# A recurrent decoder step on one core: decay by an exponential on ScalarE, gated mLSTM output in two parts, gate rows a unit later, sample tile scaled on ScalarE

## The chip, the core and the metric

The kernel runs on one core of a Trainium2 chip. The metric is the device time of one launch in microseconds. The core's engines work side by side, each through its own queue of instructions in order: TensorE (PE; its weight loads are listed as PEld), VectorE (DVE), ScalarE (ACT), GpSimd (POOL) and SyncE (SP), which here only issues transfers. They meet through semaphores: an instruction waits until a named counter has reached a value.

## The reference

One layer of a hybrid recurrent decoder for 512 prompt positions and for 8 samples of 4 positions each, 544 columns in all, in fp32. The core of it:

```
xn = rmsnorm(x, norm_mix_g);  proj = xn @ w_in + b_in      # split into q, k, v, ... gates
# GLA: chunked linear attention, decays exp(cumsum(lg)); o_gla = head_rmsnorm(o) * silu(gg)
# mLSTM: conv, silu, q/k/v block projections, stabilised memory; o_m = head_rmsnorm(hm) * sigmoid(mo)
# RG-LRU:
xc = causal_dwconv(rx);  r, i = sigmoid(blockdiag(xc, w_r) + b_r), sigmoid(blockdiag(xc, w_i) + b_i)
log_a = 8 * r * log_sigmoid(lam);  a = exp(log_a)
bx = sqrt(-expm1(2 * log_a)) * (i * xc);  h_t = a_t * h_(t-1) + bx_t;  o_r = h * gelu(ry)
mix = g0 * (o_gla @ wb0) + g1 * (o_m @ wb1) + g2 * (o_r @ wb2)      # g = sigmoid(gates)
x = x + mix @ w_out
x = x + (gelu(u_a) * u_b) @ w_down,   u = dwconv(rmsnorm(x) @ w_up)
```

The outputs are y for prompt and samples after a last RMSNorm, and the new states of every branch.

## The kernel before, in words

Activations lie with features on partitions and the 544 positions along the free axis. The dense products run as numbered **units**, one for each 128 output features: unit 0 (16 + 4 + 4 small columns: GLA rank, input and forget gates), 1 to 8 (q, k, v of GLA), 9 to 12 (mLSTM input), 13 to 20 (RG-LRU), 21 to 24 (`gg`), 25 to 28 (`mo`), 29 to 52 (gate and branch products, GLA, then RG-LRU, then mLSTM), then w_out, w_up, w_down. A unit takes fp32 products in three passes of a split in two parts: ScalarE rounds a weight tile from `stage` to `whi` (`hi`, L1060), GpSimd subtracts to get `wlo` (`lo`, L505), and TensorE adds up `whi`*`xh` + `whi`*`xl` + `wlo`*`xh` (`gemm`, L581). Two `stage` slots alternate; SyncE loads them as `lo` frees them. ScalarE evacuates each unit's result (`evac`).

The recurrent work is cut into small steps and hung between units by hand: `plan(u, part, ...)` (L303 to L341) names the steps that TensorE, ScalarE and VectorE each run when they come past unit u. Every engine runs its own function for a step, or `nothing`. Part 1 of a unit from 29 on lies between its gate product and its branch product, part 0 behind the unit.

What the change touches:

- **Start** (`start`, L595): TensorE multiplies the identity with itself 18 times, then normalises and transposes x by multiplying each token tile with a diagonal of inverse root mean squares (`normalised`, L601), for four of the eight feature tiles. The other four are scaled in place (ScalarE L1097 for token tiles 0 and 1, VectorE L1565 for 2, 3 and the 32-row sample tile 4) and transposed later (`turned`, L619). VectorE's next work is `xl` (L1572), from the `xh` that ScalarE wrote (L1109). Unit 0 (L634) follows.
- **GLA preparation** (`gprep`: VectorE L1686 to L1712, ScalarE L1188) at unit 8, with the load of the GLA states on ScalarE's queue ahead of it; **gate rows** (`rows`, VectorE L1645 to L1679) at unit 5, their store (`rowst`) at 7, their transposes (`rowt`, TensorE L666, VectorE L1681, ScalarE's exponentials L1177) at 9. The first GLA chunk (`gA`, unit 10) waits for `ke`, `cols` and `ecol`.
- **RG-LRU passes** (`rg`, i = 0 to 3, units 24, 26, 28, 30): TensorE's two gate products (L783), ScalarE two sigmoids, Tanh (L1263) and Sqrt (L1264), VectorE (`v_rg`, L1817) the decay a = (1 - t)/(1 + t) by an addition, a reciprocal and a fused pass (L1827 to L1829), then the input term, the scan and the output gate. ScalarE's sigmoids wait for the previous pass's output (`rg_o`). `mixed` (L1978, L1983) adds the branch products and comes behind the passes on VectorE's queue. The query and key projections (`mqk`, L804) wait for the convolutions and for the last state rows, all behind the passes.
- **mLSTM output** (`mfin`, L1953): in the last slot of unit 44, after the sample columns' normalised output has been copied to `mq`, VectorE multiplies each of four heads by its norm gain and `mo` (L1957), rounds it to `omh` (L1961) and subtracts to `oml` (L1962). Units 45 to 52 take k tiles one by one as `om` counts them. `omh` lies where the sample states' transposes `cts` were, so the second step waits for the last state store. The steps `sH` and `sI` (h = 0 to 3) in units 40 to 44 update the sample states. SyncE waits for `om` before it loads the residual x again (L440).

Of the kernel before, what the change touches and what calls it, by code (L numbers as in the profile page):

```python
# [57 lines left out]
WARM = 18  # L58
# [31 lines left out]
def layer(nc, io):  # L90
    ctx = ExitStack()
    with ctx:
# [58 lines left out]
        gsm = at("gsm", [P, 2, P], o + 6 * TB + 3072)  # L151
        ogh = at("ogh", [P, H, T], o, F32R)
# [32 lines left out]
        cts = at("cts", [P, NB, P + 1], w0)  # L185
        kwb = at("kwb", [TS, NB, P], w0 + 4128)
# [44 lines left out]
        m0s = sml[0:4, 196:204]  # L231

# [116 lines left out]
        def _(sp):  # L349
# [71 lines left out]
            for n in range(3):  # L421
# [143 lines left out]
        def _(pe):  # L565
# [29 lines left out]
            def start():  # L595

                pe.wait_ge(s("ident"), 1)
                for _ in range(WARM):
                    mm(bank(7)[:, 256:384], ident[:], ident[:], start=True, stop=True)
# [16 lines left out]
                pe.wait_ge(s("scaled0"), 2)  # L616
                pe.wait_ge(s("scaled1"), 3)
# [415 lines left out]
        def _(act):  # L1033
# [70 lines left out]
            hi(0)  # L1104

# [71 lines left out]
            def v_rows(_):  # L1177
# [3 lines left out]
                func(ecol[0:TS, 4, :], cols[0:TS, 4, 32:100], ACT.Exp).then_inc(s("ecol"), 1)  # L1181

# [5 lines left out]
            def v_gprep(_):  # L1188
                act.wait_ge(s("out"), outs[0])
                for h in range(H):  # L1190
                    act.dma_start(ss[64 * (h % 2):64 * (h % 2) + 64, h // 2], io["state_gla_S"][0].rearrange("b h k v -> h k b v")[h])\
                       .then_inc(s("ss_in"), 16)
# [59 lines left out]
            def v_rg(i):  # L1252
# [264 lines left out]
        def _(dve):  # L1517
# [86 lines left out]
            def v_a2(_):  # L1604
# [33 lines left out]
                v.scalar_tensor_tensor(out=c4, in0=lp, scalar=8.0, in1=lz2, op0=ALU.mult, op1=ALU.add).then_inc(s("c4"), 1)  # L1638

# [46 lines left out]
            def v_gprep(_):  # L1686

                dve.wait_ge(s("evac"), U_MU)
# [17 lines left out]
                v.tensor_tensor(qk[:, 2:4, :], qk[:, 2:4, :], g1[:], ALU.mult).then_inc(s("ke"), 1)  # L1706
                dve.wait_ge(s("ke"), 1)
# [109 lines left out]
            def v_rg(i):  # L1817
# [358 lines left out]
```

## Time and profile before

| | us |
|---|---|
| runs (median, lowest, highest of 3) | 1016.35, 1015.52, 1017.73 |
| the profiled execution | 1019.24 |
| its span, first to last instruction | 1017.5 |
| busy: TensorE, VectorE, ScalarE, GpSimd | 981.0, 588.2, 401.6, 259.4 |

The profile is one execution. Busy time of an engine is the time in which any of its instructions ran; an idle time is put down to the event that ended it ("releaser"). PEclk is the share of full clock that TensorE was granted: 1.00 is 2.4 GHz, 0.50 is 1.2 GHz. Line numbers are those of the kernel before.

### The profile page before, as it was taken

The page shows a single profiled execution, that of the slowest core. Times are in us where ns is not written, and L with a number is a line of the kernel's source. Part 1 is how long each engine was busy: PE and PEld are TensorE (multiplying, and loading weights), DVE is VectorE, ACT ScalarE, POOL GpSimd, SP SyncE. Part 2 cuts the span into 40 slices and gives each one's busy share as a digit, 9 for nine tenths or more (in the row PEclk, how much of TensorE's full clock was granted, in tenths as well). Part 3 has the DMA queues.
Part 4 walks back from the last instruction along what each step waited for, and adds up shares of the span by engine and source line. Part 5 has one row for each costly group of instructions (what it writes and reads, how often), then busy time and mean ns, then how long its engine had stood idle before and what let it go on. Part 6 is the DMA issues. An engine that isn't in the chain of part 4 may idle for free.

```text
span 1017.5 us, 19211 instructions
## 1 busy us (share of the span) xinstructions
PE 981.0 (96%) x7548; PEld 954.0 (94%) x7548; DVE 588.2 (58%) x902; ACT 401.6 (39%) x579; POOL 259.4 (25%) x145
## 2 busy tenths in 40 slices
PE   7999999998889999998999999999999999999995
PEld 7999999897789999897999999999999999999995
DVE  5484334269973555667545678776777777423132
ACT  5643333456453555222332344444444444222121
POOL 2443222232222231331433230010000100233330
PEclk8999999999999999999999999999999999999998
DMA  5236223243122222523422532233222323432212
GB/s 145 63 101 138 82 64 80 57 123 95 43 66 71 63 62 64 144 73 94 149 82 62 93 88 83 82 93 92 82 82 87 98 83 98 116 93 86 85 57 88
DMA packets 171816, 89.31 MB, mean 88 GB/s; under 512 B 13594, under 2 KB 169888, under 8 KB 171767
## 3 DMA queue, kind: packets, MB, share of 16 engines
q1 hardware_dynamic: 154341, 79.16, 28.1%
q10 hardware_dynamic: 17426, 9.47, 3.5%
q8 instruction: 35, 0.57, 0.3%
q14 instruction: 14, 0.11, 0.0%
HBM read 82.29 MB, written 6.32 MB: 87 GB/s over the span
## 4 chain that ended last, share of the span: by engine, by line
PE 84%; DVE 9%; issue 3%; ACT 1%; POOL 1%; DMA 0%; ACTq 0%; DVEq 0%; POOLq 0%
PE ps L581 74%; PE ps L570 2%; DVE rt L1828 1%; PE ps L804 1%; POOL wlo L505 1%; PE ps L885 1%; PE ps L889 1%; DVE mq L1957 1%; PE ps L634 1%; PE ps L823 1%; DVE rt L1829 1%; DMA xtok<-x_prompt 0%; DVE rt L1531 0%; PE ps L819 0%; DVE gv L1802 0%
## 5 line engine op out<-in xcount | busy, mean ns | idle before, releaser
L505 POOL TENSOR_TENSOR wlo<-stage,whi 128x1024 fp32r<-128x1024 f32 (+2 forms) x77 | 229.9, 2986 | 499.4 <-ACT whi L1060 382.1
L581 PE MATMUL ps<-xh,whi 128*128 128x272 f32 x1536 | 323.5, 292 | 3.7 <-ACT sg L1385 2.5
L581 PE MATMUL ps<-xh,wlo 128*128 128x272 f32 x1536 | 318.1, 289 | 0.0
L581 PE MATMUL ps<-xl,whi 128*128 128x272 f32 x1536 | 317.5, 288 | 0.0
L581 PEld LDWEIGHTS ps<-xh,whi 128*128 128x128 f32 x1536 | 243.1, 189 | 7.8 <-issue 4.4
L581 PEld LDWEIGHTS ps<-xl,whi 128*128 128x128 f32 x1536 | 242.2, 189 | 0.0
L581 PEld LDWEIGHTS ps<-xh,wlo 128*128 128x128 f32 x1536 | 240.5, 189 | 0.0
L1060 ACT ACTIVATE whi<-stage 128x1024 fp32r<-128x1024 f32 (+2 forms) x59 | 72.6, 1230 | 166.5 <-PE ps L581 161.2
L1069 ACT ACTIVATE whi<-stage 128x1024 fp32r<-128x1024 f32 (+1 forms) x54 | 59.9, 1110 | 145.9 <-PE ps L581 141.3
L554 POOL COPY up<-fst 128x16 f32 (+1 forms) x44 | 23.6, 538 | 231.3 <-DVE ca L2061 228.4
L2061 DVE SCALAR_TENSOR_TENSOR ca<-up,par,ca 128x560 f32<-128x560 f32 x88 | 70.3, 799 | 6.1 <-DVE ca L2061 3.2
L581 PE MATMUL ps<-hh,whi 128*128 128x272 f32 x352 | 73.5, 290 | 0.0
L581 PE MATMUL ps<-hl,whi 128*128 128x272 f32 x352 | 72.7, 287 | 0.0
L581 PE MATMUL ps<-hh,wlo 128*128 128x272 f32 x352 | 72.6, 287 | 0.0
L2051 DVE TENSOR_TENSOR wlo<-stage,whi 128x1024 fp32r<-128x1024 f32 (+1 forms) x44 | 54.7, 1244 | 10.0 <-ACT whi L1069 7.8
L2101 DVE TENSOR_TENSOR yb<-xt,ps 128x544 f32<-128x544 f32 x8 | 5.8, 721 | 88.6 <-PE ps L581 88.6
L581 PEld LDWEIGHTS ps<-hl,whi 128*128 128x128 f32 x352 | 55.5, 188 | 0.0
L581 PEld LDWEIGHTS ps<-hh,wlo 128*128 128x128 f32 x352 | 55.0, 188 | 0.0
L581 PEld LDWEIGHTS ps<-hh,whi 128*128 128x128 f32 x352 | 54.9, 188 | 0.1
L2041 DVE TENSOR_TENSOR up<-ps,rstd 128x272 f32<-128x272 f32 x44 | 19.4, 442 | 52.9 <-PE ps L581 52.9
L1385 ACT ACTIVATE sg<-ps,par 128x544 f32<-128x544 f32 x24 | 17.2, 715 | 66.7 <-PE ps L581 55.7
L1445 ACT ACTIVATE ca<-up,par 128x560 f32<-128x560 f32 x44 | 37.7, 857 | 4.0 <-DVE up L2043 2.6
(413 smaller groups left out, 1354.0 us busy)
## 6 DMA issues: line engine op xcount, KB each, us to landing
stage<-w_in SPq DMA_DIRECT2D x52, 512.0 KB, 3.9
stage<-w_up SPq DMA_DIRECT2D x44, 512.0 KB, 3.7
stage<-w_down SPq DMA_DIRECT2D x16, 704.0 KB, 4.6
stage<-w_branch SPq DMA_DIRECT2D x24, 256.0 KB, 4.2
stage<-w_out SPq DMA_DIRECT2D x8, 512.0 KB, 4.0
ch<-state_mlstm_C ACTq DMA_DIRECT2D x4, 512.0 KB, 4.1
s_mlstm_C<-ch ACTq DMA_DIRECT2D x4, 512.0 KB, 3.2
xp<-x_prompt SPq DMA_DIRECT2D x1, 2048.0 KB, 7.7
```

Source lines behind the costliest of these rows:

```text
L505: pool.tensor_tensor(wlo[:, slot, 0:kt], stage[:, slot, 0:kt], whi[:, slot, 0:kt].bitcast(F32), ALU.subtract).then_inc(s("lo"), 1)
L554: pool.tensor_copy(fsam(row[:, FPW:PADF])[:, :, 0:FW - 1], fs).then_inc(s("pads"), 1)
L570: return nc.tensor.transpose(out, in_, ident[0:k, 0:k])
L581: ins = mm(dst[:, r, :], w[:, slot, k0 + k, :], x(k)[:, r * HT:(r + 1) * HT], start=first and k == 0 and q == 0, stop=last and k == n - 1 ...
L634: ins = mm(halves(0)[:, r, :], w[:, 0, k, :], x[:, k, r * HT:(r + 1) * HT], start=k == 0 and q == 0, stop=k == KD - 1 and q == 2)
L1060: func(whi[:, slot, 0:kt], stage[:, slot, 0:kt], ACT.Copy).then_inc(s("hi"), 1)
L1069: func(whi[:, slot, 0:kt], stage[:, slot, 0:kt], ACT.Copy).then_inc(s("hi"), 1)
L1385: func(split(sg[:]), halves(0), ACT.Sigmoid, bias=col).then_inc(s("gate_ev"), 1)
L1445: func(ca[:, r, 0:CONVF], up[:, r, 0:CONVF], ACT.Identity, scale=par[:, bass.ds(j + (P_FW + NF * r), 1)], bias=par[:, bass.ds(j + (P_FB + ...
L2041: v.tensor_tensor(row[:, FW - 1:FW - 1 + HT], src[:, 0, :], rstd[:, 0:HT], ALU.mult)
L2051: v.tensor_tensor(wlo[:, slot, 0:kt], stage[:, slot, 0:kt], whi[:, slot, 0:kt].bitcast(F32), ALU.subtract)\
L2061: v.scalar_tensor_tensor(out=out, in0=row[:, t:t + CONVF], scalar=par[:, bass.ds(j + (P_FW + 2 * NF * t + NF * r), 1)], in1=out, op0=ALU.m ...
```

## The change

- Start: ScalarE scales the sample tile (`scaled(4)`, behind `hi(0)`), VectorE no longer does; TensorE multiplies the identity by itself 4 more times before the third token tile and 6 more times ahead of the last sample tile; unit 0 loads and writes 68 columns instead of 128.
- `gprep` moves from unit 8 to 5 (its first wait becomes q and k evacuated), `rows` from 5 to 6, `rowst` from 7 to 8, and the copies of sample columns become a step `smp` at unit 9. The GLA state loads move behind the exponentials of unit 9.
- RG-LRU: the decay is Exp(-2 c r) on ScalarE between Tanh and Sqrt; VectorE's addition, reciprocal and fused pass go.
- mLSTM output: the 512 prompt columns of head h are gated in a new step `mfp`, one each behind sH(0), sI(0), sH(1), sI(1); `mfin` keeps the 32 sample columns. `cts` and `kwb` move to the memory of `ogh`. `om` is counted once.

```diff
-        cts = at("cts", [P, NB, P + 1], w0)
-        kwb = at("kwb", [TS, NB, P], w0 + 4128)
+        cts = at("cts", [P, NB, P + 1], og0)
+        kwb = at("kwb", [TS, NB, P], og0 + 4128)
+        c8 = sml[:, 204:208]
...
-        plan(5, 0, ("rows", 0))
-        plan(7, 0, ("rowst", 0))
-        plan(8, 0, ("gprep", 0))
-        plan(9, 0, ("rowt", 0))
+        plan(5, 0, ("gprep", 0))
+        plan(6, 0, ("rows", 0))
+        plan(8, 0, ("rowst", 0))
+        plan(9, 0, ("rowt", 0), ("smp", 0))
...
+        for h in range(H):
+            seq[3 * NMC + 1 + h].append(("mfp", h))
...
-                    sp.wait_ge(s("om"), H)
+                    sp.wait_ge(s("om"), 1)
+                    sp.wait_ge(s("ch_out"), 64)
...
+                def warm(n, b=7):
+                    for _ in range(n):
+                        mm(bank(b)[:, 256:384], ident[:], ident[:], start=True, stop=True)
...
+                warm(18)
...
                         tr(bank(7)[:, 128:128 + KD], graw[:], KD).then_inc(s("par_tr"), 1)
+                        warm(4, 1)
                     pe.wait_ge(s("diag"), t + 1)
                     for j in range(4):
+                        if (j, t) == (3, 4):
+                            warm(6)
                         ins = normalised(j, t)
...
-                pe.wait_ge(s("scaled0"), 2)
-                pe.wait_ge(s("scaled1"), 3)
+                pe.wait_ge(s("scaled0"), 3)
+                pe.wait_ge(s("scaled1"), 2)
...
-                            ins = mm(halves(0)[:, r, :], w[:, 0, k, :], x[:, k, r * HT:(r + 1) * HT],
+                            ins = mm(halves(0)[0:68, r, :], w[:, 0, k, 0:68], x[:, k, r * HT:(r + 1) * HT],
...
-                            lambda: None, ready="om")
+                            lambda: pe.wait_ge(s("om"), 1))
...
             hi(0)
+            scaled(4)
...
                 func(ecol[0:TS, 4, :], cols[0:TS, 4, 32:100], ACT.Exp).then_inc(s("ecol"), 1)
+                act.wait_ge(s("out"), outs[0])
+                for h in range(H):
+                    act.dma_start(ss[64 * (h % 2):64 * (h % 2) + 64, h // 2], io["state_gla_S"][0].rearrange("b h k v -> h k b v")[h])\
+                       .then_inc(s("ss_in"), 16)
...
-                act.wait_ge(s("c4"), 1)
-                then(func(rt[2][:, 0:CONVM], rt[2][:, 0:CONVM], ACT.Tanh, scale=c4[:, i:i + 1]))
-                func(rt[4][:, 0:CONVM], rt[2][:, 0:CONVM], ACT.Sqrt).then_inc(s("rg_u"), 1)
+                act.wait_ge(s("c4"), 2)
+
+                func(rt[4][:, 0:CONVM], rt[2][:, 0:CONVM], ACT.Tanh, scale=c4[:, i:i + 1]).then_inc(s("rg_t"), 1)
+                act.wait_ge(s("rg_t"), 2 * i + 1)
+                func(rt[2][:, 0:CONVM], rt[2][:, 0:CONVM], ACT.Exp, scale=c8[:, i:i + 1]).then_inc(s("rg_t"), 1)
+                func(rt[4][:, 0:CONVM], rt[4][:, 0:CONVM], ACT.Sqrt).then_inc(s("rg_u"), 1)
...
+                dve.wait_ge(s("c4"), 1)
+                v.tensor_scalar(c8, c4, -2.0, None, ALU.mult).then_inc(s("c4"), 1)
...
-                dve.wait_ge(s("evac"), U_MU)
+                dve.wait_ge(s("evac"), U_QKV + 4)
...
+                dve.wait_ge(s("rg_copied"), i + 1)
+                v.tensor_tensor(h, h, xc, ALU.mult)
+                dve.wait_ge(s("rg_t"), 2 * i + 2)
                 dve.wait_ge(s("rg_u"), i + 1)
+                then(v.scalar_tensor_tensor(out=b, in0=a, scalar=1.0, in1=b, op0=ALU.add, op1=ALU.mult))
+                then(v.tensor_tensor(b, b, h, ALU.mult))
                 if i:
                     dve.wait_ge(s("or"), i)
-                then(v.tensor_scalar(r, a, 1.0, None, ALU.add))
-                then(v.reciprocal(r, r))
-                then(v.scalar_tensor_tensor(out=a, in0=a, scalar=1.0, in1=r, op0=ALU.subtract, op1=ALU.mult, reverse0=True))
-                v.tensor_tensor(h, h, xc, ALU.mult)
-                then(v.scalar_tensor_tensor(out=b, in0=b, scalar=2.0, in1=r, op0=ALU.mult, op1=ALU.mult))
-                then(v.tensor_tensor(b, b, h, ALU.mult))
...
+            def v_mfp(h):
+                if h == 0:
+                    dve.wait_ge(s("evac"), U_GB)
+                    dve.wait_ge(s("m3_copied"), NMC)
+                q = slice(0, SEQ)
+                then(gated(h, q))
+                then(v.tensor_copy(omh[:, h, q], mq[:, h, q]))
+                v.tensor_tensor(oml[:, h, q], mq[:, h, q], omh[:, h, q].bitcast(F32), ALU.subtract)
...
+                q = slice(SEQ, T)
                 for h in range(H):
-                    then(v.scalar_tensor_tensor(out=mq[:, h, :], in0=mq[:, h, :], scalar=par[:, P_MG + h:P_MG + h + 1],
-                                                in1=mo[:, h, :], op0=ALU.mult, op1=ALU.mult))
-                    if h == 0:
-                        dve.wait_ge(s("stored"), 3)
-                    then(v.tensor_copy(omh[:, h, :], mq[:, h, :]))
-                    v.tensor_tensor(oml[:, h, :], mq[:, h, :], omh[:, h, :].bitcast(F32), ALU.subtract).then_inc(s("om"), 1)
+                    ins = gated(h, q)
+                then(ins)
+                then(v.tensor_copy(omh[:, :, q], mq[:, :, q]))
+                v.tensor_tensor(oml[:, :, q], mq[:, :, q], omh[:, :, q].bitcast(F32), ALU.subtract).then_inc(s("om"), 1)
```

`gated(h, q)` is the product of L1957 on the columns q. `scaled(t)` is the copy of L1097 for token tile t.

## Rows read from the trace of the kernel before

**Rows 1.** The page's part 1: busy us, share of the span, instructions.

```profile
PE 981.0 (96%) x7548; PEld 954.0 (94%) x7548; DVE 588.2 (58%) x902; ACT 401.6 (39%) x579; POOL 259.4 (25%) x145
```

**Rows 2.** Waits of PE: line, releaser: total us, times, longest us.

```profile
PE ps L581 <- DVE mix L1983: 4.0, 1, 4.0
PE ps L804 <- issue: 3.1, 1, 3.1
PE ps L581 <- ACT sg L1385: 2.5, 1, 2.5
PE ps L581 <- DVE oml L1962: 2.2, 3, 0.9
PE ps L634 <- DVE xl L1572: 2.1, 1, 2.1
...
PE ps L570 <- ACT ecol L1181: 1.8, 1, 1.8
```

**Rows 3.** Windows: busy us (instructions) of PE, PEld, DVE, ACT, POOL; PEclk, DMA share, GB/s.

```profile
18.20:25.00 6.80, 6.80 (x29) 5.95 (x28) 2.34 (x4) 2.14 (x3) 0.93 (x5) 0.50 0.33 92
209.00:300.00 91.00, 78.17 (x551) 73.75 (x551) 84.11 (x101) 49.80 (x59) 26.32 (x9) 0.96 0.31 83
267.40:270.70 3.30, 3.30 (x14) 3.30 (x15) 2.83 (x4) 3.25 (x5) 0.00 (x0) 0.50 0.00 0
294.70:298.00 3.30, 3.30 (x10) 2.55 (x9) 3.14 (x10) 3.14 (x6) 0.00 (x0) 0.50 0.02 6
482.40:485.70 3.30, 3.30 (x15) 3.30 (x16) 1.34 (x2) 1.49 (x1) 0.03 (x1) 0.50 0.61 205
```

**Rows 4.** Timeline of the start: start us, us, engine, line, instruction [idle before <-releaser].

```profile
1.61 5.65 PE L599 MATMUL ps<-ident 128*128 128x128 f32 x36 [1.61 <-POOL ident L499]
...
13.23 2.77 DVE L1565 TENSOR_SCALAR xtok<-xtok,sml 32x512 f32<-32x512 f32 x1
13.23 2.35 POOL L505 TENSOR_TENSOR wlo<-stage,whi 128x1024 fp32r<-128x1024 f32 x1 [11.67 <-ACT whi L1060]
...
14.18 2.53 ACT L1109 ACTIVATE xh<-ps,par 128x544 fp32r<-128x544 f32 x4 [1.03 <-PE ps L603]
...
16.83 0.49 PE L634 MATMUL ps<-xh,whi 128*128 128x272 f32 x2 [2.07 <-DVE xl L1572]
```

**Rows 5.** Timeline from 58 to 93 us, VectorE and TensorE.

```profile
58.51 0.51 DVE L1647 MEMSET big<- 128x544 f32 x1
...
74.96 0.15 DVE L1679 TENSOR_TENSOR row<-rowb,row 4x8 f32<-4x8 f32 x1
83.53 4.30 DVE L1692 SCALAR_TENSOR_TENSOR qz<-qk,g 64x1088 f32<-64x1088 f32 x2 [8.42 <-ACT gv L1133]
...
87.57 0.59 PE L570 MATMUL ps<-ident,big 100*128 100x100 f32 x5
...
91.75 1.29 DVE L1706 TENSOR_TENSOR qk<-qk,g 128x1088 f32<-128x1088 f32 x1 [1.18 <-ACT g L1194]
```

**Rows 6.** Lines, 209 to 290 us, VectorE and ScalarE: count | busy us, mean ns | idle before.

```profile
L1828 DVE RECIPROCAL rt<-rt 128x568 f32<-128x568 f32 x4 | 14.8, 3703 | 0.1
L1829 DVE SCALAR_TENSOR_TENSOR rt<-rt,rt 128x568 f32<-128x568 f32 x4 | 6.1, 1532 | 0.1
...
L1264 ACT ACT_TABLE_LOAD x4 | 5.1, 1283 | 0.1
L1263 ACT ACTIVATE rt<-rt,sml 128x568 f32<-128x568 f32 x4 | 3.1, 770 | 0.1
```

**Rows 7.** Timeline from 471 to 479 us, VectorE and TensorE.

```profile
471.38 3.87 DVE L1957 SCALAR_TENSOR_TENSOR mq<-mq,par,mo 128x544 f32<-128x544 f32 x1 [0.96 <-ACT mq L1321]
...
476.40 0.78 DVE L1957 SCALAR_TENSOR_TENSOR mq<-mq,par,mo 128x544 f32<-128x544 f32 x1
...
477.22 0.41 PE L581 MATMUL ps<-omh,whi 128*128 128x272 f32 x2
...
478.33 0.78 DVE L1957 SCALAR_TENSOR_TENSOR mq<-mq,par,mo 128x544 f32<-128x544 f32 x1
```

More of the change, by code:

```diff
@@ L57 @@
 XN_PAIR = (0, 1, 2, 3, 1, 2, 3, 1)
-WARM = 18
 KT_IN, KT_GB, KT_DOWN, KT_MAX = 8, 12, 11, 12
@@ L901, in nothing @@
                 pass
-            parts = {"a2": v_a2, "csn": nothing, "decays": nothing, "rgc": nothing, "mconv": nothing, "rgd": nothing, "rows": nothing, "rowst": nothing, "rowt": v_rows, "gprep": nothing, "gA": v_gA, "gB": v_gB, "gd": v_gd, "gfin": nothing,
+            parts = {"a2": v_a2, "csn": nothing, "decays": nothing, "rgc": nothing, "mconv": nothing, "rgd": nothing, "rows": nothing, "rowst": nothing, "smp": nothing, "rowt": v_rows, "gprep": nothing, "gA": v_gA, "gB": v_gB, "gd": v_gd, "gfin": nothing,
                      "cs": v_cs, "rg": v_rg, "rh": v_rh, "gelu": nothing, "mprep": nothing, "msilu": nothing, "mqk": v_mqk, "mA": v_mA, "mB": v_mB,
-                     "mC": v_mC, "m3": v_m3, "sH": v_sH, "sI": v_sI, "sN": nothing, "mout": v_mout, "mfin": nothing}
+                     "mC": v_mC, "m3": v_m3, "sH": v_sH, "sI": v_sI, "sN": nothing, "mfp": nothing, "mout": v_mout, "mfin": nothing}
             def visit(u, part):
@@ L1092, in _, with scaled @@
             root(1)
-            for t in range(2):
+            def scaled(t):
+                n = P if t < 4 else TS
                 act.wait_ge(s("diag"), t + 1)
-                half = xtok[:, t, D_MODEL // 2:D_MODEL]
-                func(half, half, ACT.Copy, scale=mstat[:, 5 + t:6 + t]).then_inc(s("scaled0"), 1)
+                half = xtok[0:n, t, D_MODEL // 2:D_MODEL]
+                func(half, half, ACT.Copy, scale=mstat[0:n, 5 + t:6 + t]).then_inc(s("scaled0"), 1)
+            scaled(0)
+            scaled(1)
             square(2)
@@ L1188, in v_gprep @@
             def v_gprep(_):
[L1189 to L1192, printed above, removed]
                 act.wait_ge(s("db"), 1)
@@ L1365, in nothing @@
                 pass
-            parts = {"a2": v_a2, "csn": nothing, "decays": v_decays, "rgc": nothing, "mconv": nothing, "rgd": nothing, "rows": nothing, "rowst": v_rowst, "rowt": v_rows, "gprep": v_gprep, "gA": v_gA, "gB": v_gB, "gd": nothing, "gfin": v_gfin,
+            parts = {"a2": v_a2, "csn": nothing, "decays": v_decays, "rgc": nothing, "mconv": nothing, "rgd": nothing, "rows": nothing, "rowst": v_rowst, "smp": nothing, "rowt": v_rows, "gprep": v_gprep, "gA": v_gA, "gB": v_gB, "gd": nothing, "gfin": v_gfin,
                      "cs": v_cs, "rg": v_rg, "rh": v_rh, "gelu": v_gelu, "mprep": v_mprep, "msilu": v_msilu, "mqk": v_mqk, "mA": v_mA, "mB": v_mB,
-                     "mC": nothing, "m3": v_m3, "sH": v_sH, "sI": v_sI, "sN": nothing, "mout": v_mout, "mfin": v_mfin}
+                     "mC": nothing, "m3": v_m3, "sH": v_sH, "sI": v_sI, "sN": nothing, "mfp": nothing, "mout": v_mout, "mfin": v_mfin}
             def visit(u, part):
@@ L1561, in _ @@
             for t in range(2, 5):
-                n = P if t < 4 else TS
                 diagonal(t)
-                half = xtok[0:n, t, D_MODEL // 2:D_MODEL]
-                v.tensor_scalar(half, half, mstat[0:n, 5 + t:6 + t], None, ALU.mult).then_inc(s("scaled1"), 1)
+                if t < 4:
+                    half = xtok[:, t, D_MODEL // 2:D_MODEL]
+                    v.tensor_scalar(half, half, mstat[:, 5 + t:6 + t], None, ALU.mult).then_inc(s("scaled1"), 1)
                 if t == 2:
@@ L1706, in v_gprep, with v_smp @@
                 v.tensor_tensor(qk[:, 2:4, :], qk[:, 2:4, :], g1[:], ALU.mult).then_inc(s("ke"), 1)
+            def v_smp(_):
+                dve.wait_ge(s("evac"), U_MU)
                 dve.wait_ge(s("ke"), 1)
@@ L1950, in v_sI, with gated @@
                     .then_inc(s("ch_new"), 1)
+            def gated(h, cols_):
+                return v.scalar_tensor_tensor(out=mq[:, h, cols_], in0=mq[:, h, cols_], scalar=par[:, P_MG + h:P_MG + h + 1],
+                                              in1=mo[:, h, cols_], op0=ALU.mult, op1=ALU.mult)
+            def v_mfp(h):
[6 more added lines that the diff above has]
+                v.tensor_tensor(oml[:, h, q], mq[:, h, q], omh[:, h, q].bitcast(F32), ALU.subtract)
@@ L1964, in nothing @@
+                then(ins)
+                then(v.tensor_copy(omh[:, :, q], mq[:, :, q]))
+                v.tensor_tensor(oml[:, :, q], mq[:, :, q], omh[:, :, q].bitcast(F32), ALU.subtract).then_inc(s("om"), 1)
             def nothing(_):
                 pass
-            parts = {"a2": v_a2, "csn": v_csn, "decays": nothing, "rgc": v_rgc, "mconv": v_mconv, "rows": v_rows, "rowst": nothing, "rowt": v_rowt, "gprep": v_gprep, "gA": v_gA, "gB": v_gB, "gd": v_gd, "gfin": v_gfin,
+            parts = {"a2": v_a2, "csn": v_csn, "decays": nothing, "rgc": v_rgc, "mconv": v_mconv, "rows": v_rows, "rowst": nothing, "smp": v_smp, "rowt": v_rowt, "gprep": v_gprep, "gA": v_gA, "gB": v_gB, "gd": v_gd, "gfin": v_gfin,
```

6 lines of the change are left out of this document (2 added, 4 removed).

## The prediction

> **What bounds the kernel now.** I read the busy times first: TensorE's matmuls fill 981.0 of 1017.5 us, every other engine far less [rows 1]. So a saving can come only from TensorE's 36.5 idle microseconds, or from stretches that it spends at half clock. The waits of TensorE name the idle time: 4.0 us for VectorE's product at L1983, 3.1 before the query and key projections at L804, 2.5 for the gate's sigmoid at L1385, 2.2 in three pieces for the gated mLSTM rows at L1962, 2.1 for the first `xl` tile, 1.8 for `ecol` [rows 2]. Next, the clock by windows: the granted clock is 0.50 (1.2 GHz instead of 2.4) in four stretches, and TensorE is busy throughout each; each lies close behind one or more of these waits [rows 3]. A stretch of 6.80 us at half clock costs 3.4 us, one of 3.30 costs 1.65. The same view gives the widest hole: between 209 and 300 us TensorE is busy 78.17 of 91 us, so 12.8 are idle, while VectorE is busy 84.1 and ScalarE 49.8. There VectorE is the bound. The edits fall on four places, taken in order.
>
> **Start (sample tile, extra identity multiplications, 68 columns).** VectorE's scaling of the 32-row sample tile lasts 2.77 us, beginning with GpSimd's subtraction of 2.35 [rows 4]: such vector operations, with all their data in SBUF, stand until GpSimd is done. The first `xl` waits behind it on VectorE's queue, and TensorE behind that, for 2.07 us until 16.83. On ScalarE the scaling costs one short copy, bounded by the `xh` copies of 544 columns at 2.53/4 = 0.63 us; ScalarE is idle 1.03 us ahead of those [rows 4], so it costs nothing, or 0.6 if that cover is gone. `xl` then follows the first `xh`, at about 15.7. Before that TensorE has six more identity multiplications, ahead of the last sample tile. Each is two records; 36 records took 5.65 us, 0.16 each [rows 4], so 12 take 1.5 to 1.9 and end near 16.2. Gain of idle time 0.6 (0.2 to 1.1). The other four fill a wait. With the hole filled, I take the half-clock stretch behind it as gone: 3.4. Loading 68 weight columns instead of 128 I put at zero: 272 columns are still streamed, and weight loads run beside the matmuls [rows 1]; if loads set the pace it is a small gain. **Term: 4.0**, from 0.2 to 4.5.
>
> **Gate rows a unit on.** The GLA preparation moves ahead of the gate rows, the rows by one unit. The preparation took from 83.53 to 93.04, 9.5 us with one turn on ScalarE; the rows took from 58.51 to 75.11, 16.6 us [rows 5]. VectorE gets to the preparation at about 59, so the rows would end at 59 + 9.5 + 16.6 = 85.1, or 87.5 if GpSimd holds VectorE once more. TensorE wants them at 87.57 [rows 5]. The `ecol` chain behind them then has a whole unit to finish, so its wait of 1.8 goes; up to 0.9 may come back as a wait for the rows. The new wait of the moved store (`rowst`) stands on ScalarE behind unit 8; queued behind it are `hi(11)`, the evacuation of unit 9 and the exponentials. They are not wanted before TensorE's unit 11, a whole unit later. The four state loads move on ScalarE's queue behind the exponentials, beside unit 10; they are read first in unit 19. Splitting off `smp` is free, since its tiles are read in unit 18 too. **Term: 1.0**, from -1 to 1.8.
>
> **Decay from an exponential.** Each of four passes loses on VectorE a reciprocal of 3.70 us and two more passes over the tile; the fused one averages 1.53, about half of it held up by GpSimd, and I count 0.75 for it and nothing for the addition [rows 6]. That is 4.45 per pass. ScalarE gains an Exp, which the trace does not show on this tile. Its nearest row is the Tanh of the same shape, 0.77 [rows 6]. Exp also needs another table than Tanh and Sqrt may share: the Sqrt has a load of 1.28 [rows 6]. So ScalarE adds between 0.77 (no load) and 3.33 (two loads); I take one load, 2.05, as it is what the Sqrt shows. Passes are a chain (sigmoids wait for the previous pass's output, VectorE waits for ScalarE's root), so both sides count in full: 4.45 - 2.05 = 2.4 per pass, 9.6 us at its end, which is the L804 wait. TensorE has 12.8 idle us to give up there, so the 9.6 fit; about 3 of idle remain, in smaller pieces. Of the two half-clock stretches there I count one as gone, 1.65. `c8` adds one operation on four columns. What is late next is ScalarE: gates and `hi` roundings queue behind the longer pass. **Term: 11.25**, from 4.5 (two loads, 1.12 net per pass, both stretches kept) to 16 (no load, all idle and both stretches gone).
>
> By the Trainium skill, "ScalarE: Activation LUTs", section "What ACT_TABLE_LOAD costs", a change of table takes 1.28 us for the load and some 1.38 more to drain. The trace shows four loads of 1.28 with 0.1 us of idle before all of them together [rows 6], so I leave the drain out; an estimate with it is 1.38 less per pass, 5.5 us less in this term.
>
> **Prompt columns early.** Today four heads are gated in one run on VectorE once the sample columns are there. The first operation stands 3.87 us where its like takes 0.78, held up by GpSimd; heads then follow each 1.93 us; TensorE begins its first omh product at 477.22 and waits three times [rows 7], 2.2 us in all [rows 2]. Moved to the slots of `sH` and `sI` (units 40 to 42), 512 columns a head cost 4 x 1.93 = 7.7 us of VectorE, spread over two units of TensorE and more; behind them are queued the state products of `sI`, which stand for GpSimd at that time anyway. I put that at nothing, or 0 to 1 if a state product comes late. Left are four gatings, one copy and one subtraction of 32 columns a head. Tiny operations take 0.15 (L1679, [rows 5]), full ones 0.78, so 0.9 to 4; TensorE wants them at 477.22, and GpSimd lets go about 475. I take 1.2, as they are nearer the tiny ones: in time. Gain 2.2, and the half-clock stretch behind it, 1.65. SyncE's residual load waits for the same two events as before in another form, and goes out somewhat sooner; only weight tiles three units on are queued behind it. **Term: 3.85**, from 1.2 to 3.85.
>
> **Sum.** 4.0 + 1.0 + 11.25 + 3.85 = 20.1. The profiled execution took 1019.24 us (span 1017.5), so 999.1; the median of the runs, 1016.35, stands 2.9 below it, so 996.2. I say 996.
>
> **The rivals.** *ScalarE takes VectorE's place* (0.13): two loads a pass, or its longer pass delays the gates. Against it: 49.8 of 91 us busy [rows 3]. Then the decay term is 4.5, the sum 13.35, the time 1003. The skill's rule on the same page ("Table sets: the hidden batching unit") speaks against this edit: functions of one table are to be called together, and an exponential ahead of a root is its example of two loads. As a mechanism of this kernel that is the case just priced, and by the page's 2.66 us per change it would also end near 1003.
>
> *The clock is not given back* (0.09): holes close, but half-clock stretches stand elsewhere; that the extra multiplications do not do what they are there for is part of it. For: TensorE was busy all through these stretches [rows 3], so the cause is only inferred from the waits before them. Gain 0.6 + 1.0 + 9.6 + 2.2 = 13.4; 1003 again.
>
> *Rows late* (0.06): GpSimd holds VectorE in three more places at 2.35, 7 us; the rows are ready near 92, TensorE stands 4.6 in place of 1.8, and ScalarE with it. The second term becomes -2.8, the time 1000.
>
> *Slower* (0.04): the exponential's pass on ScalarE costs so much that the chain grows. It decides when the addition per pass x passes 4.45 by more than the other terms return: 4(x - 4.45) > 8.85 + 2, x > 7.2 us, an Exp and five loads. With x = 8 the time is 1016.35 - 8.85 + 14.2 = 1021.7. Nothing in the trace shows such an x; it would need VectorE and ScalarE to hold each other up.
>
> **How the numbers follow.** The forecast gets 0.68. The range reaches down to 989 (decay term near 16, the rest as taken, gives 991.4; 2 more for half-clock stretches that move) and up to 1004, past the three rivals near 1000 to 1003; outside lie the slower case and tails, under 2 in 10. With 0.2%, 2 us, as about what a measurement of this kernel can tell from no change, faster has 0.94, the same 0.02 (two rivals together), slower 0.04.
>
> **What would show it.** In the changed profile: no half clock before 30 us and `xl` at about 15.7; TensorE's `ecol` wait gone and at most 1 us for the rows; no reciprocal of 568 columns, one new load of 1.28 per pass, the L1983 wait under 1 us and the L804 wait under 3; no wait for `oml` after the first omh product, and no half clock behind it. The forecast is wrong if TensorE waits as long for ScalarE in units 27 to 33 as it did for VectorE, or if half-clock time stays near what it is.

## The result, and the profile after

The changed kernel takes 999.49 us, the median of 4 runs (998.65 to 1000.70), beside 1016.41 for the kernel before: ratio 0.9833, 95% interval 0.9816 to 0.985. That is 17 us saved, where 20 were forecast. The profiled execution took 1000.22 us (span 998.5, mean granted clock 0.991; before 1019.24, 1017.5 and 0.982).

The busy times come first, as in [rows 1]:

```profile
PE 975.5 (98%) x7568; PEld 951.0 (95%) x7568; DVE 577.8 (58%) x896; ACT 410.1 (41%) x588; POOL 259.8 (26%) x145
```

TensorE's idle time fell from 36.5 to 998.5 - 975.5 = 23.0 us, 13.5 less. Its busy time fell by 5.5 as well, although it has 20 records more (the ten extra multiplications): fewer of its records ran at half clock (27 us in seven stretches before, 10 in three after, the last 12 us of either span left out). So 13.5 + 5.5 = 19.0 us of span. The waits of TensorE, beside [rows 2]:

```profile
PE ps L814 <- issue: 3.1, 1, 3.1
PE ps L793 <- ACT rout L1249: 2.7, 1, 2.7
...
PE ps L574 <- DVE row L1699: 1.2, 1, 1.2
```

The product's 4.0, the sigmoid's 2.5, the gated rows' 2.2, the `xl` tile's 2.1 and the 1.8 for `ecol` are gone. The 3.1 ahead of the query and key projections (L804, now L814) are all still there; new are 1.2 for the gate rows, and the wait of the third pair of gate products for `rout`, ScalarE's copies of the convolution states, has grown from 0.9 to 2.7. The windows, beside [rows 3] (busy us of PE, PEld, DVE, ACT, POOL; granted clock, DMA share, GB/s):

```profile
18.20:25.00 6.80, 6.80 (x54) 6.18 (x53) 3.92 (x5) 3.60 (x5) 1.70 (x6) 1.00 0.32 85
209.00:300.00 91.00, 84.31 (x616) 79.98 (x616) 74.41 (x93) 60.91 (x70) 28.77 (x10) 1.00 0.32 87
86.30:89.70 3.40, 3.40 (x16) 3.40 (x16) 3.04 (x5) 1.68 (x7) 2.37 (x1) 0.50 0.32 78
434.50:437.85 3.35, 3.35 (x17) 3.35 (x16) 1.56 (x3) 0.00 (x0) 0.00 (x0) 0.50 0.21 66
```

The start and the wide hole run at full clock; TensorE works 84.31 of 91 us in the hole, not 78.17. Behind the wait for the gate rows there is a new stretch at half clock; the one at 434.5 has its like at 448 before the change.

**Start.** The timeline, beside [rows 4]:

```profile
13.27 2.35 POOL L509 TENSOR_TENSOR wlo<-stage,whi 128x1024 fp32r<-128x1024 f32 x1 [11.72 <-ACT whi L1070]
13.38 0.72 ACT L1108 ACTIVATE xtok<-xtok,sml 32x512 f32<-32x512 f32 x1 [0.19 <-DVE dt L1571]
...
14.50 1.61 PE L603 MATMUL ps<-ident 128*128 128x128 f32 x12
...
15.05 2.96 DVE L1590 SCALAR_TENSOR_TENSOR xl<-ps,par,xh 128x544 fp32r<-128x544 f32 x4 [1.71 <-ACT xh L1124]
...
16.37 0.47 PE L644 MATMUL ps<-xh,whi 128*68 128x272 f32 x2
```

ScalarE scales the tile in 0.72 us while GpSimd subtracts, and `xl` is begun at 15.05. The first unit begins only at 16.37 (16.83 before), since the six multiplications now stand ahead of it. The 68 columns show no difference: six products of unit 0 take about 0.75 us at full clock in both kernels.

**Gate rows.** The timeline around them, beside [rows 5]:

```profile
67.93 0.51 DVE L1667 MEMSET big<- 128x544 f32 x1
...
84.33 0.15 DVE L1699 TENSOR_TENSOR row<-rowb,row 4x8 f32<-4x8 f32 x1
...
84.54 0.65 PE L574 MATMUL ps<-ident,big 100*128 100x100 f32 x5 [1.23 <-DVE row L1699]
```

The rows are ready at 84.5; TensorE wanted them at 83.3, not at 87.57.

**Decay.** The lines from 205 to 280 us, beside [rows 6] (count | busy us, mean ns | idle before, releaser):

```profile
L1857 DVE COPY rt<-sml 128x8 f32<-128x8 f32 x4 | 9.0, 2248 | 0.2
L1281 ACT ACT_TABLE_LOAD x4 | 5.1, 1283 | 0.1
L1281 ACT ACTIVATE rt<-rt,sml 128x568 f32<-128x568 f32 x4 | 3.1, 771 | 0.0
L1851 DVE SCALAR_TENSOR_TENSOR rt<-rt,rt 128x568 f32<-128x568 f32 x4 | 3.0, 750 | 4.5 <-ACT rt L1282 4.5
```

The exponential costs one load of 1.283 and 0.771 us a pass. The addition, the reciprocal and the fused pass of 1.53 are gone; L1851 is another fused operation, which stands for the one at L1831 and waits 4.5 us in all for the root. GpSimd's hold has moved and grown: a copy of eight columns (L1857) now stands 2.25 us on average, 0.95 with the old decay (e1), 0.16 when it is free.

**Prompt columns.** The timeline, beside [rows 7]:

```profile
458.03 3.49 POOL L509 TENSOR_TENSOR wlo<-stage,whi 128x1536 fp32r<-128x1536 f32 x1 [12.71 <-ACT whi L1070]
458.14 3.91 DVE L1976 SCALAR_TENSOR_TENSOR mq<-mq,par,mo 128x32 f32<-128x32 f32 x4 [0.88 <-ACT mq L1339]
462.36 0.29 DVE L1996 TENSOR_TENSOR oml<-mq,omh 128x128 fp32r<-128x128 f32 x1
462.70 0.52 PE L585 MATMUL ps<-omh,whi 128*128 128x272 f32 x2
```

The four small gatings take 3.91 us, because the first stands until GpSimd lets go; the last row is ready at 462.65, and TensorE takes it at 462.70 without a wait that the profile shows.

### The profile page after: what moved, and what is told of

Same layout as the page of the kernel before. It is cut to its first block, busy times and chain, and to the rows that moved or that the text cites. A ratio compares the mean times of both kernels' runs of the same rounds, so it can differ in the third digit from the quotient of the medians.

```text
span 998.5 us, 19261 instructions
## 1 busy us (share of the span) xinstructions
PE 975.5 (98%) x7568; PEld 951.0 (95%) x7568; DVE 577.8 (58%) x896; ACT 410.1 (41%) x588; POOL 259.8 (26%) x145
## 4 chain that ended last, share of the span: by engine, by line
PE 86%; DVE 8%; ACT 3%; issue 2%; ACTq 0%; POOL 0%; DVEq 0%; POOLq 0%
PE ps L585 74%; PE ps L574 3%; PE ps L603 1%; PE ps L814 1%; PE ps L895 1%; PE ps L899 1%; PE ps L644 1%; DVE rt L1857 1%; PE ps L833 1%; PE ps L610 0%; PE ps L829 0%; DVE bc L1631 0%; DVE gv L1825 0%; ACT whi L1070 0%; PE ps L840 0%
```

## The experiments

All edits are to the changed kernel, and all ratios are to the kernel before. An interval is about 0.25% to either side, so a difference of two of them carries some 3 us: the decay and the prompt columns can be sized by time alone, the smaller parts only with their traces.

**e1, the decay undone.** ScalarE's and VectorE's `v_rg` are those of before:

```diff
-func(rt[4][:, 0:CONVM], rt[2][:, 0:CONVM], ACT.Tanh, scale=c4[:, i:i + 1]).then_inc(s("rg_t"), 1)
...
-func(rt[2][:, 0:CONVM], rt[2][:, 0:CONVM], ACT.Exp, scale=c8[:, i:i + 1]).then_inc(s("rg_t"), 1)
-func(rt[4][:, 0:CONVM], rt[4][:, 0:CONVM], ACT.Sqrt).then_inc(s("rg_u"), 1)
+then(func(rt[2][:, 0:CONVM], rt[2][:, 0:CONVM], ACT.Tanh, scale=c4[:, i:i + 1]))
+func(rt[4][:, 0:CONVM], rt[2][:, 0:CONVM], ACT.Sqrt).then_inc(s("rg_u"), 1)
...
+then(v.reciprocal(r, r))
```

> The changed kernel with the old decay (reciprocal form) back; all else as changed. Theory: this part is worth 9.4 us (TensorE's lead over the kernel before grows from 3.4 us ahead of the passes to 11.5 at its query and key projections, with one half-clock stretch of 1.7 gone behind them, less a little), so 999.5 + 9.4 = 1009 us, ratio to the kernel before 0.993. Rival, ScalarE takes VectorE's place: worth 4.5, 1004 us, ratio 0.988.

1009.57 us, ratio 0.9927 (0.9903 to 0.995): the part is worth (0.9927 - 0.9833) x 1016.4 = 9.6 us, with some 3 us to either side. TensorE's waits in this run:

```profile
PE ps L585 <- DVE mix L2013: 3.9, 1, 3.9
PE ps L814 <- issue: 3.1, 1, 3.1
PE ps L585 <- ACT sg L1400: 2.5, 1, 2.5
PE ps L574 <- ACT rt L1274: 1.7, 1, 1.7
...
PE ps L793 <- ACT rout L1249: 0.9, 1, 0.9
```

The idle time that the new decay saves is the product's 3.9, the sigmoid's 2.5 and 1.7 ahead of the states' transposes, less the 1.8 by which the wait for `rout` grows: 6.3 us. The wait at L814 is the same with either decay. The rest of the gain is the clock; the window of e1, beside that of the changed kernel above:

```profile
209.00:300.00 91.00, 78.19 (x559) 74.17 (x558) 82.52 (x101) 48.96 (x57) 26.75 (x9) 0.96 0.30 77
```

Two half-clock stretches, at 264 and 291 us, are back, and cost 3.4 us together. The executions of e1 that the ratio rests on list clocks of 0.984 to 0.989, those of the changed kernel 0.988 to 0.994 (e12 included), which fits. ScalarE's first sigmoid in passes 2 to 4, in e1 and then in the changed kernel, shows what one pass gains (pass 1 begins at 211.15 and 211.24):

```profile
227.67 0.73 ACT L1273 ACTIVATE rt<-ps,par 128x568 f32<-128x568 f32 x1 [6.33 <-DVE rt L1858]
...
245.41 0.74 ACT L1273 ACTIVATE rt<-ps,par 128x568 f32<-128x568 f32 x1 [5.55 <-DVE rt L1858]
...
264.50 0.73 ACT L1273 ACTIVATE rt<-ps,par 128x568 f32<-128x568 f32 x1
```

```profile
225.77 0.73 ACT L1273 ACTIVATE rt<-ps,par 128x568 f32<-128x568 f32 x1 [3.75 <-DVE rt L1862]
...
239.94 0.72 ACT L1273 ACTIVATE rt<-ps,par 128x568 f32<-128x568 f32 x1
...
257.43 0.73 ACT L1273 ACTIVATE rt<-ps,par 128x568 f32<-128x568 f32 x1
```

The first three passes are 2.0, 3.6 and 1.6 us shorter, and from the fourth's sigmoid to the copy `hrow` of the last state row (290.02 in e1, 281.96 in the changed kernel) it is 1.0: 8.15 us in all.

**e2, the prompt columns undone.** `mfin` gates whole heads again, with its tiles where they were:

```diff
-seq[3 * NMC + 1 + h].append(("mfp", h))
...
-cts = at("cts", [P, NB, P + 1], og0)
+cts = at("cts", [P, NB, P + 1], w0)
...
+then(v.scalar_tensor_tensor(out=mq[:, h, :], in0=mq[:, h, :], scalar=par[:, P_MG + h:P_MG + h + 1],
+                            in1=mo[:, h, :], op0=ALU.mult, op1=ALU.mult))
```

> The changed kernel with the four heads of the matrix-memory output gated in one run at the end again. Theory: worth 4.0 us, 2.2 of idle time on TensorE and one half-clock stretch of 3.4 (1.7) behind the waits, so 1003.5 us, ratio 0.9873, and the profile shows both again. Rival, only the idle time comes back and the clock stays at 1.00: 2.2, 1001.7.

1004.61 us, ratio 0.9884 (0.9857 to 0.991): 5.2 us, above both theories' values, though the interval holds 4.0. A line of its waits, and a window of the kernel before, say why it is more than 2.2:

```profile
PE ps L582 <- DVE oml L1981: 3.3, 4, 0.9
```

```profile
468.80:472.10 3.30, 3.02 (x14) 2.88 (x15) 2.30 (x4) 2.38 (x4) 0.93 (x1) 0.50 0.49 159
```

TensorE now waits for all four heads. In the profiled execution of the kernel before it ran at half clock just ahead of them and came to them 5.84 us after the first gating began; in e2 it comes after 4.60 and stands 0.66 us for the first head too. Between 462 and 470 us its clock stays at 1.00 in this trace; half-clock stretches stand at 86, 284 and 421 us. So the half-clock share of the term was not seen where I had placed it, and of the 5.2 us only 3.4 stand as idle time in the profiles (26.4 us against 23.0).

**e3, the rows ahead of the preparation again, its shorter wait kept.**

```diff
-plan(5, 0, ("gprep", 0))
-plan(6, 0, ("rows", 0))
-plan(8, 0, ("rowst", 0))
+plan(5, 0, ("rows", 0))
+plan(7, 0, ("rowst", 0))
+plan(8, 0, ("gprep", 0), ("smp", 0))
...
```

> The changed kernel with the gate rows ahead of the GLA preparation again, and the four state loads where they were. Theory: as changed, the rows' wait of 1.23 us and the half-clock stretch behind it (1.7) ate what the vanished wait of 1.8 gave, so this run is the same as the changed one within 0.5 us: 999.5, ratio 0.9833. Rival, the forecast's own term: 1.0 us slower, 1000.5. A third: the rows' new place harms, and this run is 1 us faster.

The four state loads go back too. 998.01 us, ratio 0.9824 (0.9798 to 0.9851), on the side of the third theory, but not apart from the changed kernel by time. The trace is clear: TensorE waits neither for the rows nor for `ecol`. The timeline of VectorE in this run:

```profile
71.74 0.15 DVE L1699 TENSOR_TENSOR row<-rowb,row 4x8 f32<-4x8 f32 x1
71.83 4.68 DVE L1712 SCALAR_TENSOR_TENSOR qz<-qk,g 64x1088 f32<-64x1088 f32 x2
...
85.15 0.24 DVE L1704 COPY cols<-ps 32x100 f32<-32x100 f32 x1
```

The preparation begins as soon as the rows are done, and the columns behind it are copied by 85.4.

**e8, the same with the longer wait too.** This undoes the whole part:

```diff
+plan(5, 0, ("rows", 0))
...
-dve.wait_ge(s("evac"), U_QKV + 4)
+dve.wait_ge(s("evac"), U_MU)
```

> The changed kernel with the gate-row part fully undone: rows ahead of the GLA preparation, and that preparation waiting for the value projections' evacuations again. Run e3 kept the preparation's shorter wait and had no wait of TensorE there at all. Theory: it is the shorter wait, not the order, that removed the ecol wait; so here the wait of 1.8 us is back, and the time is 1.8 us or, with a half-clock stretch, 3.5 above e3: 999.8 to 1001.5. Rival: the earlier start alone removed it, and the time is that of e3, 998.0.

1000.91 us, ratio 0.9843 (0.9819 to 0.9868): the whole part is worth 1.0 us, less than the uncertainty of some 3. A wait of 1.8 us for `ecol` is back, and VectorE's timeline shows its source:

```profile
79.17 4.30 DVE L1712 SCALAR_TENSOR_TENSOR qz<-qk,g 64x1088 f32<-64x1088 f32 x2 [7.10 <-ACT gv L1148]
...
91.70 0.24 DVE L1704 COPY cols<-ps 32x100 f32<-32x100 f32 x1
```

VectorE stands 7.10 us for the evacuation of the last values, which the preparation's first products do not need. The columns queued behind it come at 91.9, 6.5 us later than in e3. So the shorter wait removes the wait for `ecol`; beside it the new order removes nothing, and brings the wait for the rows.

**e4, the start undone.**

```diff
-warm(4, 1)
...
-warm(6)
...
-scaled(4)
...
+v.tensor_scalar(half, half, mstat[0:n, 5 + t:6 + t], None, ALU.mult).then_inc(s("scaled1"), 1)
...
-ins = mm(halves(0)[0:68, r, :], w[:, 0, k, 0:68], x[:, k, r * HT:(r + 1) * HT],
+ins = mm(halves(0)[:, r, :], w[:, 0, k, :], x[:, k, r * HT:(r + 1) * HT],
```

> The changed kernel with the start as before: the sample tile scaled on VectorE, no extra identity multiplications, 128 weight columns. Theory: worth 3.6 us, nearly all of it the half-clock stretch of 6.8 us (3.4) that comes back with the 2 us hole ahead of the first unit: 1003.1 us, ratio 0.9869. Rival, the clock stays as it is and only the idle time counts: 0.5, 1000.

1002.05 us, ratio 0.9864 (0.9834 to 0.9895): 3.2 us. The wait of 2.07 for `xl` is back, and a window shows the half clock behind it:

```profile
16.50:23.20 6.70, 6.33 (x26) 5.58 (x27) 3.08 (x5) 1.68 (x3) 2.23 (x11) 0.50 0.29 73
```

The trace of this run shows one thing more, in the rows around the gate rows:

```profile
87.47 0.15 DVE L1695 TENSOR_TENSOR row<-rowb,row 4x8 f32<-4x8 f32 x1
...
87.67 0.65 PE L574 MATMUL ps<-ident,big 100*128 100x100 f32 x5
```

With the late start the rows are ready at 87.62, and TensorE comes to them at 87.67 and waits for nothing. In the changed kernel the rows are 3.1 us sooner (84.48) and TensorE 4.3 (83.3): the wait of 1.2 is there because the faster start brings TensorE further forward than the rows.

**e5, only the extra multiplications away.**

```diff
-warm(4, 1)
...
-warm(6)
```

> The changed kernel without the ten extra identity multiplications; the sample tile stays on ScalarE. Theory: they are what keeps the clock up at the start, so a half-clock stretch of 6.8 us comes back behind the hole: about 3 us slower than the changed kernel, 1002.5 us, ratio 0.9863. Rival: with the sample tile off VectorE the hole is too short to matter, and the six multiplications ahead of the last tile only delay the first unit (16.37 in the changed kernel): 0 to 1 us faster, 998.5 to 999.5.

1000.91 us, ratio 0.9849 (0.982 to 0.9879): 1.6 us slower than the changed kernel, between the two theories, and by time apart from neither. TensorE's timeline and a window of it:

```profile
15.96 0.43 PE L641 MATMUL ps<-xh,whi 128*68 128x272 f32 x2 [1.19 <-DVE xl L1587]
```

```profile
17.70:21.00 3.30, 3.30 (x16) 2.90 (x15) 1.16 (x3) 1.27 (x2) 1.34 (x6) 0.50 0.13 39
```

Without them the first unit begins 0.4 us sooner, behind a hole of 1.19, and 3.4 us at half clock follow, which cost 1.7: 1.3 net. So in these traces the scaling on ScalarE halves the hole and the half-clock stretch (6.8 in e4), and the multiplications remove the rest. In all eleven traces of kernels that have both, the clock is 1.00 from 9 to 30 us.

**e6, a Tanh in place of the Exp.** This leaves out the exponential, and with it its table load:

```diff
-func(rt[2][:, 0:CONVM], rt[2][:, 0:CONVM], ACT.Exp, scale=c8[:, i:i + 1]).then_inc(s("rg_t"), 1)
+func(rt[2][:, 0:CONVM], rt[2][:, 0:CONVM], ACT.Tanh, scale=c8[:, i:i + 1]).then_inc(s("rg_t"), 1)
```

> The changed kernel with a Tanh in place of the Exp in the four gate passes, so without the Exp's table load (it leaves out the exponential; the rest is as changed). Forecast's theory, the pass is a chain in which ScalarE's time counts in full: 4 x 1.28 = 5.1 us faster than the changed kernel, 994.4. Rival: VectorE, which GpSimd holds up in every pass, and the state rows on ScalarE set the end, and the load is mostly hidden: at most 2 us faster, 997.5 or more.

994.22 us, ratio 0.9785 (0.9763 to 0.9808): 5.3 us below the changed kernel by the medians, 4.9 by the ratios, beside 4 x 1.28 = 5.1. The rival falls, but the theory does not hold in every pass. From first sigmoid to first sigmoid (209.77, 223.11, 236.03, 253.54) the first two passes are 1.19 and 1.25 us shorter than in the changed kernel, the third not at all, and the fourth 1.28 to its output: in the third VectorE, held by GpSimd, comes to L1851 behind the root in both kernels (at 247.46 in the changed one, where the root ends at 246.16). Up to `hrow` the passes gain 4.3 us. This execution also begins them 1.5 us sooner, without the half-clock stretch at 86 us, so a part of the 5.3 is the clock. The wait for `rout` shrinks to 0.4, that at L814 to 2.0.

**e7, the second silu behind the state row.**

```diff
-plan(31, 0, ("msilu", 0), ("msilu", 1), ("mconv", 1), ("mconv", 2), ("mconv", 3))
-plan(32, 1, ("rh", 0), ("msilu", 2), ("msilu", 3), ("mprep", 0))
+plan(31, 0, ("msilu", 0), ("mconv", 1), ("mconv", 2), ("mconv", 3))
+plan(32, 1, ("rh", 0), ("msilu", 1), ("msilu", 2), ("msilu", 3), ("mprep", 0))
```

> The changed kernel with the second silu of the convolved rows moved behind the state row's copy on ScalarE's queue (from unit 31 to unit 32). Theory: the wait of 3.07 us at the query and key projections stands for that copy, which is queued behind the second silu and a gate with a table load each, not for the decay; with the copy ahead of them it falls below 0.5, so 2.6 to 3.1 us faster: 996.4 to 996.9, and 1.7 more where a half-clock stretch followed. Rival: the next wait, for the gate of unit 33 or the silus, takes its place: at most 1 us faster.

995.71 us, ratio 0.9805 (0.9782 to 0.9828): 3.8 us below the changed kernel by the medians, 2.8 by the ratios. First the timeline of the changed kernel at this place, then that of e7:

```profile
279.29 0.63 ACT L1297 ACTIVATE mcv<-rt 128x512 f32<-128x512 f32 x1 [6.25 <-DVE rt L1549]
...
281.96 0.57 ACT L1287 ACTIVATE hrow<-ps 9x512 f32<-9x512 f32 x1
...
282.63 2.07 PE L814 MATMUL ps<-mcv,wq 128*128 128x272 f32 x8 [3.07 <-issue]
```

```profile
276.73 0.57 ACT L1287 ACTIVATE hrow<-ps 9x512 f32<-9x512 f32 x1
...
277.91 2.00 PE L814 MATMUL ps<-mcv,wq 128*128 128x272 f32 x8
```

In the changed kernel ScalarE idles 6.25 us for the second convolution, then runs its silu, a gate with its table load (1.28) and the small copy `hrow`, for which TensorE waits. With the silu moved, the copy is done at 277.3 and TensorE begins without a wait. 1.2 us come back later, in two waits.

**e10, the convolution states' transposes and copies at unit 23 in place of 27.**

```diff
-plan(27, 0, ("cs", 0), ("cs", 1))
+plan(23, 0, ("cs", 0), ("cs", 1))
...
-pe.wait_ge(s("rg_copied"), 2)
+pe.wait_ge(s("ss_new"), 2)
+pe.wait_ge(s("t3_copied"), NCH + 1)
...
+pe.wait_ge(s("state_rows"), 2)
...
-if i == 2:
-    pe.wait_ge(s("state_rows"), 2)
```

> The changed kernel with the two convolution states' transposes and copies at unit 23 in place of 27, alone. Theory: TensorE's wait of 2.66 us at the third pair of gate products is for these copies, which are queued behind a gate pass on ScalarE; without it TensorE gains 2.66 there, and keeps it if the last pass does not end later: 996.8 us, ratio 0.9807. Rival: the passes are the chain, TensorE merely waits later (for the fourth pass at unit 30, or the query and key projections), and the time stays within 1 us: 998.5 to 999.5.

TensorE's wait for the copies moves with them, from the third pair of gate products to the first. 1005.49 us, ratio 0.9894 (0.9865 to 0.9923), 6 us slower: neither theory. The wait of 2.66 is gone, and 4.3 stand at the gate of unit 30. First GpSimd and VectorE in the changed kernel, then in e10:

```profile
233.46 3.49 POOL L509 TENSOR_TENSOR wlo<-stage,whi 128x1536 fp32r<-128x1536 f32 x1 [8.51 <-ACT whi L1070]
...
237.02 1.34 DVE L1858 TENSOR_TENSOR_SCAN rt<-rt,rt 128x568 f32<-128x568 f32 x1
```

```profile
233.09 6.93 POOL L509 TENSOR_TENSOR wlo<-stage,whi 128x1536 fp32r<-128x1536 f32 x2 [8.52 <-ACT whi L1070]
233.32 3.27 DVE L1857 COPY rt<-sml 128x8 f32<-128x8 f32 x1
236.63 4.58 DVE L1858 TENSOR_TENSOR_SCAN rt<-rt,rt 128x568 f32<-128x568 f32 x1
```

Without the copies ScalarE rounds the next weights 3 us sooner, so GpSimd runs two subtractions back to back, and the scan, which slipped between them, is held for the second. The next sigmoids begin at 242.27 in place of 239.94, and the gate behind that pass is late. TensorE's idle time is 3.3 us above the changed kernel's in these traces, and behind the wait of 4.3 the clock is 0.50 from 251.4 to 254.7 us, which costs 1.65; the rest of the 6 us is not placed.

**e9, e3, e7 and e10 together.**

> The changed kernel with three things: the gate rows ahead of the GLA preparation again but with the preparation's shorter wait (as e3), the second silu behind the state row's copy (as e7), and the two convolution states' transposes and copies at unit 23 in place of 27, ahead of the gate passes. Theory, the holes are separate: e3 gave 0.9 to 1.5 us, e7 2.8 to 3.8, and the wait of 2.66 us for those copies goes too; 999.5 - 1.2 - 3.3 - 2.7 = 992.3 us, ratio 0.976. Rival, the third edit only lets TensorE wait for the gate passes instead: 995, ratio 0.979.

998.84 us, ratio 0.9816 (0.9787 to 0.9845). Above both theories: the wait of 4.3 us at the gate of unit 30 is here as well, so the third edit takes back what the other two gain.

**e11 and e12: e3 and e7 together, beside the changed kernel.**

> The changed kernel with the gate rows ahead of the GLA preparation again (shorter wait kept, as e3) and the second silu behind the state row's copy (as e7), without the states' move that e10 showed to harm. Theory, e9 was slow only by that move: the gains of e3 (0.9 to 1.5) and e7 (2.8 to 3.8) add up, 999.5 - 4.3 = 995.2 us, between 994 and 996, ratio 0.979 to 0.980. Rival: an earlier TensorE meets GpSimd's holds elsewhere in the gate passes as in e10, and the time is 998 or more.

> The changed kernel once more, as it stands, beside e11 on one chip, so that the two compare directly: 999.5 us, ratio 0.9833, within 0.2%.

e11 takes 993.93 us, ratio 0.9786 (0.9762 to 0.981); the changed kernel, on the same chip, 998.7, ratio 0.9832 (0.9807 to 0.9856). The two edits add up to some 4.7 us and make the best version of these: 2.1% under the kernel before.

## Why the prediction was right, and where its steps were off

The forecast (996, with 989 to 1004) holds: all four parts gain, the decay most. It was 3.5 us too low. Of the rivals, ScalarE did not take VectorE's place (no gate waits for its longer pass; only the wait for `rout` grew, by 1.8), the clock was given back in good part (27 us of half clock became 10), and the late rows came in small, 1.2 us of wait in place of 4.6. By its steps, with each part's worth from the runs without it:

| part | forecast | measured (parts: some 3 us to either side) |
|---|---|---|
| start | 4.0 | 3.2 |
| gate rows | 1.0 | 1.0 |
| decay | 11.25 | 9.6 |
| prompt columns | 3.85 | 5.2 |
| all together | 20.1 | 17 |

The parts sum to 19.0, within their uncertainty of the whole.

**Decay.** The price on ScalarE held: 2.05 us a pass, a load of 1.283 and an Exp of 0.771. Three steps were wrong, and the agreement of the measured 9.6 with the forecast's 4 x 2.4 is luck.

VectorE's side was mispriced both ways. The addition, put at nothing, took 0.45 us a pass in e1, and the gate's product at L1848, which no step counts, now runs in three of the passes while VectorE would wait for the root. Against that, GpSimd's holds grew: in e1 VectorE is busy only 10.6 us more than in the changed kernel, though the reciprocal, the fused pass and the addition there last 22.7 together.

"Both sides count in full" failed: the passes gain 2.0, 3.6, 1.6 and 1.0 us, 8.15 in place of 9.6, and the third is not shortened by a load less on ScalarE (e6). TensorE's idle time between 209 and 300 us fell by 6.1, not by 9.6 (12.8 in e1, 6.7 as changed), and the clock gave back both half-clock stretches, 3.4, not one of 1.65. The two errors nearly cancel: 6.1 + 3.4 = 9.5.

"At its end, which is the L804 wait": that wait did not move, and e1 and e7 show that it stands for a small copy in ScalarE's queue. The idle time came out of the waits at L1983 and L1385, and a wait that the profile puts down to "issue" had not been followed to its semaphore. So "the L804 wait under 3" failed (3.1), while "the L1983 wait under 1" held.

By the Trainium skill, "ScalarE: Activation LUTs", section "What ACT_TABLE_LOAD costs", a change of table takes a drain of 1.38 us beside the load of 1.28. The trace agrees with the load (1.283) and not with the drain: 0.1 us of idle ahead of all four, and in e6 a load less shortened a pass by 1.19 to 1.28 us where it counted, not by 2.66.

**Gate rows.** The size agrees, but its uncertainty is three times as large, and the steps to it were off. The rows came at 84.5, near the 85.1 forecast, from a preparation that began at 56.2 in place of 59 and took 11.7 in place of 9.5. "TensorE wants them at 87.57" left out that the start brings TensorE there sooner: it came at 83.3, and waited 1.2 us, where "at most 1 us" was a sign of being right, with a half-clock stretch behind it in the profiled execution. e4 shows no such wait at the old start. And "the `ecol` chain then has a whole unit to finish" credits the order; e3 and e8 show that the preparation's wait for the values was what held the columns back.

**Start.** The hole and the half-clock stretch went as forecast. Of the idle time 0.46 us came back, as the multiplications, at 1.61 us, end at 16.1, where I had them, and set the first unit. `xl` came at 15.05, sooner than the 15.7 forecast, and that helped nothing.

**Prompt columns.** "1.2, as they are nearer the tiny ones" was wrong: the four gatings alone took 3.91 and all six operations 4.51, past the bound's far end of 4, since GpSimd holds the first. They are just in time, with nothing to spare. The term itself was too small: the trace of before shows 2.2 us of waits where TensorE came to the heads 1.2 us later, behind a half-clock stretch; without the edit it now waits for four heads, 3.3 us. The 1.65 for the clock behind them is not seen in e2.

**The sum.** Between the two profiled executions the gain is 19.0 us, 1.1 under the forecast; between the medians it is 16.9. So some 2 us of the miss come from the execution that I had read: it lay 2.8 us above the median, where the one after the change lies 0.7 above its own, and its listed clock is 0.982 where a median execution has 0.985 to 0.986. I took the gain from it and applied it to the median. "Four stretches" at half clock was a miscount as well: this execution has three more, at 418, 448 and 469 us, one of which hid a part of the wait for the heads, and two of which have their likes after the change, at 404 and 434.5. The idle terms sum to 13.4 (0.6 + 1.0 + 9.6 + 2.2), and 13.5 were measured, though part by part they were off. No experiment isolates the clock's share.

## What to carry to other kernels

Price each edit at the moment when the others have moved its consumer: an earlier start made the rows late, and an earlier rounding put a scan behind GpSimd. Before moving a late step, look whether a wait ahead of it on its queue asks for more than its reader needs; shortening that wait did here what the reordering was meant to do. A stall put down to "issue" is to be followed to its semaphore and to the queue of the engine that raises it, and half-clock stretches are to be counted over several executions before they stand in a sum. Where a measured part equals its forecast, look at its pieces all the same: the decay's 9.6 was two errors that cancel.

## What the runs showed of the hardware

The same kernel does not fall to half clock behind the same waits in each execution. A window of e12, which is the changed kernel once more:

```profile
86.30:89.70 3.40, 3.40 (x29) 3.40 (x28) 2.96 (x5) 1.58 (x7) 2.40 (x1) 1.00 0.28 68
```

TensorE waited 1.22 us for the rows here too, yet the stretch behind runs at full clock, with 29 matmul records in place of 16. This execution has one such stretch inside, the first one three, and it took 995.69 us where that took 1000.22. Thirteen executions of the kernel before on one chip went from 1011.36 us at a mean granted clock of 0.989 to 1019.99 at 0.980, about 1 us for each 0.001; the profiled one had 0.982, a median one 0.985 to 0.986.

GpSimd's subtraction holds small operations too: the copy of eight columns at L1857 took 0.16 us alone and 3.28 beside it, and a scan that begins just ahead of a second subtraction took 4.58 in place of 1.34.
